# Two expert pieces staged and copied on chip, other homes for cross-attention tiles, and the first expert unit on half the gather

## The reference, cut to what matters

```
h = h + _mixer(...)                       # first block
h = h + _cross_attention(h, mem, ...)
h = h + _hier_moe(h, ...)
x = hybrid_layer(x, mem_2, ...)           # second block

# _hier_moe, for each token: one of 4 groups, then the two best of its 8 experts
hid = silu(xb @ w_gate[e]) * (xb @ w_up[e])      # w_gate, w_up: 32 x 1024 x 512
y   = hid @ w_down[e]                            # w_down: 32 x 512 x 1024
```

## Time and profile before

| | |
|---|---|
| time, median of 3 executions | 1053.41 us (1052.27 to 1054.94) |
| time of the profiled execution | 1052.48 us |
| its span | 1050.7 us |
| TensorE busy | 869.0 us, 83% |
| VectorE busy | 457.0 us, 43% |
| ScalarE busy | 322.1 us, 31% |
| read from memory | 290.25 MB, 277 GB/s over the span |
| mean granted TensorE clock | 0.921 of full speed |
| chain that ended last | issue 31%, PE 30%, DMA 26%, SPq 7%, DVE 4% |

### The profile page before, as it was taken

The page is one execution under the profiler, slowest core; times in us unless marked ns, Lnnn a source line. Parts: engine busy times, 40 slices in busy tenths (PEclk is TensorE's granted clock), DMA queues, the critical chain, the costliest instruction groups (busy, mean ns, idle before and its releaser), DMA issues.

```text
span 1050.7 us, 13600 instructions
## 1 busy us (share of the span) xinstructions
PE 869.0 (83%) x5499; PEld 605.5 (58%) x5499; DVE 457.0 (43%) x849; ACT 322.1 (31%) x520; POOL 23.6 (2%) x34
## 2 busy tenths in 40 slices
PE   8999999999966575756656657656999999999996
PEld 8877888898612131312213122212788899999985
DVE  5668766674602020201102011101766788665684
ACT  4656654764000000000001000001444555445332
POOL 1020010100000000000000000000000000000000
PEclk9999999999989788888878778879999999999998
DMA  9552465556999999999999999999355344444441
GB/s 308 183 162 82 160 220 208 186 186 254 344 423 419 422 422 422 422 421 423 421 422 422 421 419 420 421 421 404 113 164 188 129 161 144 139 161 133 148 161 41
DMA packets 72828, 292.10 MB, mean 278 GB/s; under 512 B 6370, under 2 KB 6852, under 8 KB 48708
## 3 DMA queue, kind: packets, MB, share of 16 engines
q1 hardware_dynamic: 70708, 289.53, 71.3%
q10 hardware_dynamic: 2064, 1.79, 0.5%
HBM read 290.25 MB, written 1.05 MB: 277 GB/s over the span
## 4 chain that ended last, share of the span: by engine, by line
issue 31%; PE 30%; DMA 26%; SPq 7%; DVE 4%; ACT 1%; POOL 0%; DVEq 0%; POOLq 0%; ACTq 0%
DMA ring<-in_w_e_down 12%; DMA ring<-in_w_e_up 7%; SPq L598 7%; PE bank L2208 6%; PE bank L2210 5%; PE bank L2209 5%; DMA ring<-in_w_e_gate 5%; PE bank L2570 4%; PE bank L2585 3%; DMA ring<-in_w_in 2%; PE bank L2547 1%; PE bank L2145 1%; DVE ring_rounded L1296 1%; ACT ring_rounded L809 1%; PE bank L2613 1%
## 5 line engine op out<-in xcount | busy, mean ns | idle before, releaser
L1296 DVE TENSOR_TENSOR ring_rounded<-ring,ring_rounded 128x2048 fp32r<-128x2048 f32 x80 | 183.3, 2291 | 135.0 <-ACT ring_rounded L809 134.7
L809 ACT ACTIVATE ring_rounded<-ring 128x2048 fp32r<-128x2048 f32 x80 | 153.2, 1915 | 197.8 <-PE bank L2210 196.5
L2570 PE MATMUL bank<-ring,main 128*32 128x512 f32 x768 | 115.8, 760 | 65.7 <-DMA ring<-in_w_e_up 50.6
L2209 PE MATMUL bank<-ring_rounded 128*128 128x256 f32 (+1 forms) x512 | 158.4, 309 | 0.0
L2210 PE MATMUL bank<-ring_rounded 128*128 128x512 f32 x368 | 144.4, 392 | 0.0
L2570 PEld LDWEIGHTS bank<-ring,main 128*32 128x32 f32 x768 | 27.9, 135 | 150.5 <-issue 71.7
L2585 PE MATMUL bank<-ring,main 128*32 128x512 f32 x384 | 64.6, 831 | 49.3 <-DMA ring<-in_w_e_down 49.3
L2208 PE MATMUL bank<-uT_rounded,ring_rounded 128*128 128x256 f32 x352 | 101.8, 289 | 0.4 <-issue 0.4
L2209 PEld LDWEIGHTS bank<-ring_rounded 128*128 128x128 f32 x512 | 97.6, 191 | 4.8
L1821 DVE TENSOR_TENSOR h<-bank,h 128x512 f32<-128x512 f32 x32 | 22.0, 690 | 178.8 <-PE bank L2613 178.8
L2210 PE MATMUL bank<-uT_rounded,ring_rounded 128*128 128x256 f32 x352 | 99.5, 283 | 0.0
(11 more groups left out here) (287 smaller groups left out, 1263.7 us busy)
## 6 DMA issues: line engine op xcount, KB each, us to landing
ring<-in_w_e_gate SPq DMA_DIRECT2D x48, 1024.0 KB, 26.4
ring<-in_w_e_up SPq DMA_DIRECT2D x48, 1024.0 KB, 26.7
ring<-in_w_in SPq DMA_DIRECT2D x46, 1024.0 KB, 5.0
ring<-in_w_e_down SPq DMA_DIRECT2D x44, 1024.0 KB, 26.2
main<-in_w_e_up SPq DMA_DIRECT2D x12, 1024.0 KB, 26.8
main<-in_w_e_gate SPq DMA_DIRECT2D x12, 1024.0 KB, 26.7
main<-in_w_e_down SPq DMA_DIRECT2D x12, 1024.0 KB, 25.7
ring<-in_w_ckv SPq DMA_DIRECT2D x8, 1024.0 KB, 5.0
```

The lines of the kernel that those rows point to most:

```text
L809: a.activation(rounded(hi_half(h)), raw_half(name, h), ACT.Copy).then_inc(hi_made, 1)
L1296: v.tensor_tensor(rounded(raw), raw, as_f32(hi_half(h)), ALU.subtract).then_inc(split_made, 1)
L2209: mm(dst, left[0], right[1], start=False, stop=False, skip_group_check=True)
L2570: last = mm(bank[2 + part][on, :], xg3[:, h * (KC // 2) + k, on], weight_unit(unit_buffer(p, u), e, KC)[:, k, :], start=h + k == 0, stop=h ...
```

## The change

1. Homes. `coT` (turned output of the cross-attention) moves from `main` to `lo_b`; the low part of the second memory moves from `lo_b` to a new place `mem2_lo` in `main`; the probability tiles and `cq_tok`, `cqT` move inside `main`. So `cq_tok` and `cqT` now lie exactly on the pieces 0 and 1 of buffer 2, and piece 3 of buffer 3 (`lo_b`) is free once co1 is done.
2. Order on SyncE. Pieces of the first four units are issued at other places of the list (below).
3. Staging. The first halves of the down weights of experts 0 and 1 (pieces 0 and 1 of unit 4 of quad 0) are loaded in two transfers of 512 KB each into free places (`main[:, 5376:6400]` and `squares` for expert 0, `mem2T` for expert 1), ahead of the point at which their buffer is free. ScalarE copies them into buffer 0 after unit 0 has been used (`place_staged`, four copies of 128x1024), between the copy of the turned gates and the tanh of the first quad. For that the first quad is taken out of ScalarE's loop.
4. Half the gather. A new semaphore `gathered_lo` is raised when the first four chunks are gathered; ScalarE copies them at that point. Unit 0 waits only for that copy, unit 1 for VectorE's, and the two transposes of the gates stand behind unit 0 (`turn_gates`), in every quad.

```diff
             for name in FIRST_BLOCKS[2:]:
+                if name == "xv2":
+                    wait_filled(sp, "co_3")
+                    load_unit(0, (GROUP - 1,), gate_w_of, 0, at=GROUP - 1)
                 load_dense(name)
...
                     load_unit(2, (2,), up_w_of, 0, at=2)
+                    sp.wait_ge(head_summed, len(HEAD_SQUARES))
+                    load_staged(0)
+                    wait_filled(sp, "cqT3")
+                    load_unit(2, (0,), up_w_of, 0)
                     wait_filled(sp, "cs1_1")
                     load_unit(0, (2,), gate_w_of, 0, at=2)
-
-            wait_filled(sp, "co_3")
-            load_unit(0, (GROUP - 1,), gate_w_of, 0, at=GROUP - 1)
-            load_unit(2, (0, 1), up_w_of, 0)
+                    load_unit(2, (1,), up_w_of, 0, at=1)
+
+            wait_used(sp, "co1", 0)
+            load_unit(1, (0,), gate_w_of, 1)
             wait_filled(sp, LAST_USE["co1"])
-            load_unit(1, (0, 1), gate_w_of, 1)
-            load_unit(3, (2,), up_w_of, 1, at=2)
+            load_unit(1, (1,), gate_w_of, 1, at=1)
+            load_unit(3, (2, 3), up_w_of, 1, at=2)
...
             load_unit(3, (1,), up_w_of, 1, at=1)
-            load_unit(3, (3,), up_w_of, 1, at=3)
-            load_quad(0, 0, range(GROUP), range(UNIT_BUFFERS, UNITS))
+            load_staged(1)
+            sp.wait_ge(moe.unit_used, 1)
+            load_unit(0, (2, 3), down_w_of, 0, FC, at=2)
+            load_quad(0, 0, range(GROUP), range(UNIT_BUFFERS + 1, UNITS))
             load_quad(0, 1, range(GROUP, 2 * GROUP))
...
+            def place_staged():
+
+                act.wait_ge(moe.unit_used, 1)
+                for i in range(2):
+                    act.wait_ge(staged_landed[i], 16 * 2)
+                    for k in range(2):
+                        ins = a.activation(weight_unit(0, i, FC)[:, k, :], staged[i][k], ACT.Copy)
+                    ins.then_inc(unit_landed[0], 16)
```

More of the change, by code:

```diff
@@ L326, in build @@
         c = Carver(main, 0, main_cols)
-        cq_tok, cqT, coT = c.take(2048), c.take(2048), c.take(2048)
-        c_prob = [c.take(512) for _ in range(4)]
+        c_prob = [c.take(512) for _ in range(3)]
+        c.at = 1792
+        mem2_lo = c.take(2048)
+        c_prob += [c.take(512)]
         c_pT = [c.take(512) for _ in range(2)]
+        c.at = 6400
+        cq_tok, cqT = c.take(2048), c.take(2048)
         ck_tok = normed[:, :, :].rearrange("p t d -> p (t d)")
@@ L356, in build @@
         spare_at = c.at
-        assert spare_at >= experts_end + 512
+        assert spare_at >= experts_end + 512 and spare_at == 6400
         dq2T, dk2T = c.take(1024), c.take(1024)
@@ L365, in build @@
         mem2T = main[:, c.at:c.at + 2048]
+        staged = [[main[:, 5376:6400], squares[:, :]], [mem2T[:, 0:1024], mem2T[:, 1024:2048]]]
         score = c.take(384)
@@ L421, in build @@
         moe = ExpertSems(sem, "moe")
+        staged_landed = [sem(f"staged_piece_landed{i}") for i in range(2)]
         last_landed = [sem(f"last_unit_chunk_landed{k}") for k in range(2)]
@@ L616, in load_quad, with load_staged @@
                         load_unit(unit_buffer(p, u), experts, w_of, u % 2, chunks)
+            def load_staged(i):
+                for k in range(2):
+                    sp.dma_start(staged[i][k], down_w_of[i, :, k, :]).then_inc(staged_landed[i], 16)
             for name in FIRST_BLOCKS[2:]:
+                if name == "xv2":
+                    wait_filled(sp, "co_3")
+                    load_unit(0, (GROUP - 1,), gate_w_of, 0, at=GROUP - 1)
                 load_dense(name)
@@ L1084, in gathered_low, with act_quad @@
             def gathered_low(S, n):
-                act.wait_ge(S.gathered, n + 1)
+                act.wait_ge(S.gathered_lo, n + 1)
                 a.activation(xgT[:, 0:512], bank[0][:, :], ACT.Copy).then_inc(S.lo_drained, 1)
             a.activation(act_junk[:, :], bias[:, 0:1], ACT.Copy).then_inc(moe.y_ready, 1)
-            def act_quad(n):
+            def place_staged():
+                act.wait_ge(moe.unit_used, 1)
+                for i in range(2):
+                    act.wait_ge(staged_landed[i], 16 * 2)
+                    for k in range(2):
+                        ins = a.activation(weight_unit(0, i, FC)[:, k, :], staged[i][k], ACT.Copy)
+                    ins.then_inc(unit_landed[0], 16)
+            def act_quad(n, first=False):
                 gathered_low(moe, n)
                 expert_gates(moe, n)
+                if first:
+                    place_staged()
                 expert_tanh(moe, n)
@@ L1094, in act_quad @@
                 expert_out(moe, n)
-            with act.Fori(0, 2 * LAST_PAIR) as n:
+            act_quad(0, first=True)
+            with act.Fori(1, 2 * LAST_PAIR) as n:
                 act_quad(n)
@@ L2527, in rank_tokens @@
                     full("rank", mm(b[:, 2 * NE:3 * NE], ones[:, :], assigned[:, 1, :], start=False, stop=True))
-            moving("xv2", parts(mem2T, lo_b), rank_tokens)
+            moving("xv2", parts(mem2T, mem2_lo), rank_tokens)
             def wait_last_uses(banks):
@@ L2548, in gather, with turn_gates @@
                                   stop=t == TT - 1)
+                    if k == KC // 2 - 1:
+                        last.then_inc(S.gathered_lo, 1)
                 last.then_inc(S.gathered, 1)
-            def experts(S, j, p, final=False):
+            def turn_gates(S, j, p):
                 pe.wait_ge(S.gates_ready, of_quad(j, p, 1, 1))
@@ L2565, in experts @@
                         u = 2 * part + h
+                        if part == 0:
+                            pe.wait_ge((S.lo_drained, S.hi_drained)[h], of_quad(j, p, 1, 1))
                         pe.wait_ge(unit_landed[unit_buffer(p, u)], landed_count(j, p, u))
```

11 lines of the change are left out of this document (7 added, 4 removed).

## The result

The changed kernel ran at a median of 1045.6 us (1045.34 to 1048.55, 5 runs) against 1053.56 us for the kernel before; the ratio is 0.9933, with a 95% interval of 0.9918 to 0.9949. The quotient of the two medians alone would be 0.9924. That is faster, and exactly on the lower end of the range that was forecast (1045.6 to 1051.2, with 1048.4 as the likeliest). Two more sets of runs of the same kernel gave 0.9954 (0.9936 to 0.9972) and 0.9941 (0.9922 to 0.9960). The profiled execution took 1048.42 us with a span of 1046.7 us.

A forecast was written before the change was run, and what follows sets the result against it. The full transfer queue in the quads was taken as the bound. Two pieces fewer at 2.49 us, with copies, half the gather and holes at 0, gave 1053.41 - 4.98 = 1048.4 us, range 1045.6 to 1051.2.

The forecast's parts named there:

- What bounds the kernel: In the quads the transfer queue is full for 17 slices at 419 to 423 GB/s; pieces left at 278 us decide.
- The staged pieces, 2 x 2.49 = 4.98 us: At 278 us 177 pieces are left in place of 179, each 2.49 us, so 4.98 us less.
- No new hole: Behind 286.7 us, units 4 and 5 are issued in time; a hole is bounded by 0 and 1 us, taken as 0.
- the 400 that I gave as the sign: From 280 to 300 us no stretch of 1 us falls under 400 GB/s.
- The copies, hidden: Four ScalarE copies in quad 0, 4.2 us, move the tanh from 288.86 to near 292.2 us and cost nothing.
- Half the gather, nothing at the end: Unit 0 starts 0.9 us earlier, worth 0 to the end; it helps only the cover of unit 4's issue.
- Homes, nothing: No gain was counted for the new homes; the reordering on the dense path costs nothing, bounded by 0 and 1 us.
- The small transfers: Rival: halves of the second staged piece each pay 2 us in series, 4 us of gain lost, 1052.4 us; chance 0.04.
- The tanh: Rival: quad 0's tanh waits for the staged piece, free up to about 19 us of delay, near 1057 us; chance 0.03.
- Everything behind the quads moves as it is: Behind the quads nothing changes, since its weights queue behind the last expert piece; about 321 us of span remain.
- the fall as a rival on the slow side alone: Rival: the full queue starts late, also by half clock outside the quads, or a hole opens; 1050.4 us or more; chance 0.13.
- the likeliest case: The queue starts at 278 us with 177 pieces left: 1048.4 us, within 1046.0 to 1050.5; chance 0.8.

The follow-up runs named there:

- 175 with a hole: The changed kernel with pieces 2 and 3 of unit 4 of quad 0 loaded only in their first 64 columns: 1044.09 us, ratio 0.9919.
- the order alone: The changed kernel without staging, all four pieces of unit 4 loaded behind unit 0, homes and half the gather kept: 1051.3 us, ratio 0.9979.
- one piece staged: The changed kernel with expert 0's piece staged and expert 1's loaded with pieces 2 and 3 of unit 4 behind unit 0: 1048.95 us, ratio 0.9955.

## Why the prediction was right, and where it was short

- **What bounds the kernel.** Right, though I miscounted the slices: 16 of them, from 289 to 709 us, have 419 to 423 GB/s, and the 17th has 404. The time from the gather to the last half unit follows the pieces left: 452.6 us for 179, 447.7 for 177, 444.9 for 175 with a hole.
- **The staged pieces, 2 x 2.49 = 4.98 us.** Right: 452.57 - 447.76 = 4.81 us in the first pair of profiles, 4.87 against the second one. But the working took the gain from the count of pieces alone (15 issued before 277 us where there were 13), and did not say that the staged piece of expert 1 is needed as a filler. The runs show it: without it 2.0 us are lost.
- **No new hole.** Right for the change; the lowest stretch from 280 us on has 381 GB/s. That is under the 400 that I gave as the sign, but the sign was set too tight: the kernel before has stretches of 356 and 385 GB/s there too. The bound of 1 us for a hole, had there been one, was too small: with the order alone and with one piece staged 2.1 and 2.0 us were lost. With the order alone unit 4 is issued at 283.38 us, and the rate is back over 350 GB/s only in the stretch from 286.
- **The copies, hidden.** Right, with 2.0 us of delay of the tanh for the 3.3 that I had.
- **Half the gather, nothing at the end.** Right, shown both ways.
- **Homes, nothing.** Wrong by a little: 0.3 us ahead of the quads by the profiles, and by the ratios some 1 us more, whose cause is open.
- **The rivals.** The small transfers overlapped: 4.8 of the 4.98 us came. The tanh waited 2.5 us for the staged piece and started 2.0 us later than before, far from the 19 at which it would decide. The Trainium skill (DMA: Bandwidth & Descriptors, Anatomy of one DMA) has a fixed 2.0 us for each transfer, for the path through GpSimd. Paid in series it would have left an estimated gain of 1.1 us; the trace, with 4.8 us, doesn't agree with that for queued transfers.
- **"Everything behind the quads moves as it is."** This is the step that failed in size. It took TensorE's clock at the end of the quads and behind them as given. It stood at half over the last half unit of the profiled execution (1.5 us lost), and other executions of the same kernel have no fall, or one elsewhere. The prediction had the fall as a rival on the slow side alone, and let the profiled execution of before stand for all, though it held one fall and the second profile of the same program held three. It also took falls to be as frequent in both kernels, and the homes' surplus of about 1 us speaks against that.
- **The median.** 1045.6 us lies 2.8 us under the forecast, on the very end of the range and outside the 1046.0 to 1050.5 that I gave for the likeliest case; the end itself, 1045.6, was reached by no working. That this set holds is luck, though the two later sets lie well inside. Of the 2.8 us, 0.3 are the homes. The later sets of the same kernel stand at 1047.6 and 1047.8 us, so some 2 us lay in the executions of the first set, and the 0.3 to 0.5 us left over lie within the homes' surplus. Their spans say what they were: the three quick ones have 1043.6, 1043.7 and 1043.9 us, and the second profile of the change, 1045.0 us with one fall of 1.2 us, would have 1043.8 without it. So they most likely had no fall. Their mean clock fits (0.924 to 0.929, against 0.919 and 0.916 in the others), but no profile of one of them exists.

## What to carry to other kernels

When a stage is one full transfer queue, count the transfers left at the instant it becomes full, and ask for each edit whether that count falls and whether the queue stays full behind it. A piece that is only moved forward can be lost again in a hole: here one piece forward was worth 0.3 us of the queue's time without a filler, and a staged piece behind it was worth 2 us although it changed no count. And cut several profiles of each kernel at the same instants before reading a difference of 1 or 2 us in the whole.

## What the runs showed that I had not expected

- **The clock's falls are worth 1.2 to 1.7 us each and change from one execution to the next.** Falls to 0.50 (1.2 GHz) that cost time lay at 12 to 16 us (1.2 us of cost), at 262 to 267 us (1.6 us), at the last half unit (1.5 to 1.7 us) and at 732 to 745 us (1.4 us). The 14 profiles held one to three of them, never both of the first two. Ahead of the last half unit stood idle time of TensorE of 3.05 to 3.20 us in profiles with a fall there. But 3.34 us stood there in the kernel before, and 3.19 and 3.20 us in two others, without a fall. Falls inside the quads, while TensorE waits for transfers anyway, show no cost: the second profile of the change has one from 713 to 719 us, and its 447.70 us to the last half unit are as in the first.
- **A matmul's pace changed with the place that its standing operand comes from.** In co0 and co1 128x512 matmuls take 0.231 us from start to start with that operand in `main` and 0.227 in `ring`, at a full and at an idle queue. In the last part of xv2, with the low part moved the other way, it is 0.232 before and 0.233 after. What makes it so wasn't looked into.
